# Two experts' endings rewritten: TensorE's branch moved ahead of them, the last half summed in PSUM, the first one's affine moved to other engines

## The chip, the core and the metric

One core of a Trainium2 chip runs one program with five engines: TensorE (PE, matmuls, results in PSUM), VectorE (DVE), ScalarE (ACT), GpSimd (POOL) and SyncE (SP, here the issuer of most DMAs). The time is device microseconds of one execution; the median over several runs counts. Weights stream from HBM during the whole program.

## The reference

Two hybrid layers (four mixers side by side) come first, then two blocks of attention and mixture of experts. All is in float32, for 256 tokens of 1024 channels. The change lies in the second part:

```python
x = layer_norm(DEEPNORM_ALPHA * x + (1 + g1) * y, ln_g[i, 0], ln_b[i, 0])   # y: attention (i=0 neighbourhood, i=1 grouped)
h = x * (1 + sc2) + sh2
y = hierarchical_moe(h, ...)            # 32 experts, 2 of them per token
x = layer_norm(DEEPNORM_ALPHA * x + (1 + g2) * y, ln_g[i, 1], ln_b[i, 1])
...                                     # the next block begins with
h = x * (1 + sc1) + sh1                 # sc1, sh1, g1: rows of mod = silu(c) @ ada_w[i] + ada_b[i]
y = gqa_mixer(h, ...)                   # q, k, v = h @ w_qkv; rms norm, rope, attention, w_o
```

`layer_norm` takes mean and variance over the 1024 channels, then `(x - mean) * rsqrt(var + 1e-5) * g + b`.

## The kernel before

Each engine has its program written out by hand, in the order in which it runs; semaphores (`filled(...)`: a PSUM result is there; `drained(...)`: it has been read and its bank is free) join them. The 256 tokens are two tiles (`t` = 0, 1) of 128 partitions, X[:, t, :]. There are 8 PSUM banks of 512 columns; `begin(b, name)` waits until bank b is free.

The 32 experts of a block run in 8 rounds (`q`) of four (`experts`). A round gathers up to 32 tokens for each expert, multiplies with gate and up (L920), transposes the hidden values (`hidden`), multiplies with the down weights, scales with the gate row g2 on VectorE (`YS`, L1062) and scatters the sums back to the tokens with a matmul (`combine`, L983) that VectorE adds to ACC, which is X. In the last round of a block the down weights come in five pieces: three rows f of four experts (`down_rows`, L965) and the two halves of the last row (`down_end`, L973). Between them TensorE spreads the gain and the shift of the layer norm over the partitions (`norm_row`, L888: a matmul of one row of ones), ScalarE copies them to `LN_OUT`. VectorE then adds the last sums to X, takes the statistics (BATCH_NORM_STATS2, `stats`), GpSimd computes the inverse root (L2261) and VectorE applies mean, root, gain and shift in four passes of 1024 columns (`last_norm`, L1070).

Should an expert get more than 32 tokens, `overflow` computes the rest. It stands under an `If` on the largest count (`cnt`): the engine loads the number (TENSOR_LOAD) and branches. `overflow` isn't entered for these inputs, but its code lies between: 32 experts written out. TensorE meets this `If` after the ending; VectorE before its own ending, which stands there twice (once with `overflow`, once in `Else`).

The grouped attention of the second block follows the first block's ending. TensorE first spreads the gate row g1 (`gate_rows`, L493, called by `common(1, "g")`), transposes X (`norm_cols`, L449), and once ScalarE (`early_cols`) and VectorE (`last_cols`) have scaled and shifted the transposed columns into `HT`, it multiplies with the keys' and the queries' weights: `k0` (L453, keys of tile 0), then `k1`, `q00`, transposes `K0`, `K1`, then `q10`, `r00` and the first scores. GpSimd computes the inverse roots of the keys' and queries' norms (`ROPED`). SyncE loads all large weights, each piece into the slot of an older one, after that has been used.

Of the kernel before, what the change touches and what calls it, by code (L numbers as in the profile page):

```python
# [9 lines left out]
ALU = mybir.AluOpType  # L10
# [4 lines left out]
NT = 2  # L15
# [113 lines left out]
def program(nc, A, out):  # L129
    with ExitStack() as ctx:  # L130
# [303 lines left out]
        def _(eng):  # L434
# [371 lines left out]
            def grouped():  # L806
# [83 lines left out]
            def experts(i):  # L890
# [12 lines left out]
                for q in range(NQ):  # L903
# [52 lines left out]

                    def down_rows():
                        o = [begin(5 + n, "dn", i, q, n) for n in range(2)]
                        for j in range(4):
                            pe.wait_ge(*drained("aT", i, q, j))  # L960
                        for f in range(3):
                            pe.wait_ge(*loaded("dn", i, q, "row", f))
                            for n in range(2):
                                for j in range(4):
                                    ins = eng.matmul(o[n][32 * j:32 * j + 32, :], AT[u][:, j, 32 * f:32 * f + 32],  # L965
                                                     rows_of_four(i, f)[:, j, 512 * n:512 * n + 512], start=f == 0, stop=False)
# [3 lines left out]
                    def down_end(o, n):  # L970
                        pe.wait_ge(*loaded("dn", i, q, "end", n))
                        for j in range(4):
                            ins = eng.matmul(o[n][32 * j:32 * j + 32, :], AT[u][:, j, 96:128], ends_of_four(i, n)[:, j, :],  # L973
                                             start=False, stop=True)
                        end(ins, "dn", i, q, n)
                        DONE["dn", i, q, "end", n] = filled("dn", i, q, n)

# [8 lines left out]
                    if q == NQ - 1:  # L986
# [6 lines left out]
                    else:  # L993
                        down(0)
                        down(1)
                        combine(0)
                    combine(1)
# [48 lines left out]
            for i in range(DEPTH):  # L1046
# [6 lines left out]
                pe.wait_ge(sem("cnt"), i + 1)  # L1053
                with eng.If(eng.value_load(cnt[0:1, NE:NE + 1]) > CAP):
                    overflow(i)

        @block.vector
        def _(eng):
# [392 lines left out]
            def last_cols():  # L1451
                v.wait_ge(*filled("nT", 1, 1, 1))
                for a in range(4):
                    c = 4 + a
                    ins = ts(HT[:, c, 128:256], bank("nT", 1, 1, 1)[:, 128 * a:128 * a + 128],
                             mod[:, 1, 8 + c:9 + c], ALU.mult, mod[:, 1, c:c + 1], ALU.add)
                    if a == 3:
                        free(ins, "nT", 1, 1, 1)
# [3 lines left out]
            def norm_columns(n, i, k):  # L1462
# [6 lines left out]
                v.tell(tt(COMB[:, n, 1], COMB[:, n, 1], sh, ALU.add), sem("comb"), i + 1)  # L1469
# [41 lines left out]
            def out_quarter(i, t, q):  # L1511
                o, f = slice(256 * q, 256 * q + 256), f"o{t}{q}"
                v.wait_ge(*drained("g1", i, 0))
                v.wait_ge(*drained("g1", i, 1))
                v.wait_ge(*filled(TAG[i], f))
# [13 lines left out]
            def side(i, tokens, more):  # L1529
                for f in tokens:  # L1530
# [11 lines left out]
                    elif kind == "n":  # L1542
                        norm_columns(2 * i, i, 3)
# [19 lines left out]
            def neighbourhood():  # L1563
# [11 lines left out]
                norm_columns(0, 0, 3)  # L1575
# [6 lines left out]
            def grouped():  # L1582
                last_cols()
# [7 lines left out]

# [129 lines left out]
            def experts(i, chosen):  # L1721
# [17 lines left out]
                for q in range(NQ):  # L1739
# [8 lines left out]
                    for j in range(4):  # L1748
# [25 lines left out]
                        if not q:  # L1774
                            extract(10 + i)
                            gate_rows(2 + i)
                    v.wait_ge(*filled("gsT", i, q))
# [37 lines left out]
                    def end():  # L1815
                        for n in range(2):
                            down(n)
                            combine(n)
# [3 lines left out]
                    kept = v.n, dict(v.past), v.last  # L1822
                    with eng.If(eng.value_load(cnt[0:1, NE:NE + 1]) > CAP):
                        end()
                        overflow(i)
                    v.n, v.past, v.last = kept
                    with eng.Else():
                        end()
# [40 lines left out]
            def last_norm(i):  # L1869
                for t in range(NT):  # L1870
                    deviation(t)
                for n in range(2):
                    for h in range(2):
                        v.wait_ge(*drained("row", 2 * i + 1, n, h))
                for t in range(NT):
                    v.step(stt(X[:, t, :], X[:, t, :], bn_a[:, t, 0:1], LN_OUT[0], ALU.subtract, ALU.mult))
                v.chain()
                for t in range(NT):
                    v.wait_ge(sem("lrs"), n_dev[0] - 1 + t)
                    ins = stt(X[:, t, :], X[:, t, :], st2[:, t:t + 1], LN_OUT[1], ALU.mult, ALU.add)  # L1880
                    if i + 1 < DEPTH:
# [717 lines left out]
```

## Time and profile before

| | us |
|---|---|
| median of 3 runs (lowest, highest) | 1532.74 (1531.36, 1538.42) |
| the profiled execution's own time | 1536.27 |
| its span | 1534.5 |
| TensorE busy | 1376.1 (90%) |
| VectorE, ScalarE, GpSimd busy | 547.8, 218.1, 85.4 |
| moved by DMA | 531.23 MB, mean 346 GB/s |

The span is cut by the page into 40 slices. In slices 15 to 23 and 31 to 38, in the two blocks' experts, DMA is full at about 426 GB/s, and the time goes with the weights; in between, in the attention of the second block (about 930 to 1070 us), DMA falls as low as 106 GB/s and TensorE and VectorE set the pace. The first experts' ending is at 905 to 934 us, the second one's at 1500 to 1531 us, where the program ends.

### The profile page before, as it was taken

Reading aid. Unit: us, or ns where it says so; the run is one execution under the profiler, and the core shown is the slowest. Engines: PE = TensorE matmul, PEld = TensorE weight load, DVE = VectorE, ACT = ScalarE, POOL = GpSimd, SP = SyncE. Lnnn points to the kernel's source line nnn. Section 1 sums busy time; section 2 is a strip of 40 time slices with the busy share of each in tenths; the row PEclk is TensorE's granted clock in tenths of the full one; section 3 lists DMA queues with packets and bytes.
Section 4 is the critical chain, followed back from the end, with each engine's and each line's share of the span. In section 5 each row is a group of like instructions: output and inputs, shape, how many; then the busy total and the mean of one; then the engine's idle time right before and its main releaser. Section 6 shows DMA issues by size and latency. Waiting matters only on the chain.

```text
span 1534.5 us, 28540 instructions
## 1 busy us (share of the span) xinstructions
PE 1376.1 (90%) x12866; PEld 874.1 (57%) x12866; DVE 547.8 (36%) x1251; ACT 218.1 (14%) x578; POOL 85.4 (6%) x91
## 2 busy tenths in 40 slices
PE   7999999999999998879879788878999798798796
PEld 4886488578886555436435443467665363354451
DVE  3596659665843221111111105583211111111113
ACT  3230123022332000000000001442100000000000
POOL 3100111000003000000000001100200000000000
PEclk9999999999999999889889999989999898898997
DMA  9657945778869999999999997237999999999994
GB/s 345 225 195 261 333 171 202 285 267 306 311 270 353 421 427 426 428 426 425 428 426 426 427 399 278 106 121 316 423 410 426 426 426 428 427 426 426 428 420 178
DMA packets 94552, 531.23 MB, mean 346 GB/s; under 512 B 5184, under 2 KB 7424, under 8 KB 70608
## 3 DMA queue, kind: packets, MB, share of 16 engines
q1 hardware_dynamic: 91264, 519.40, 83.8%
q0 software_dynamic: 3152, 9.86, 1.9%
q8 instruction: 105, 1.72, 0.4%
q14 instruction: 31, 0.25, 0.0%
HBM read 528.19 MB, written 1.05 MB: 345 GB/s over the span
## 4 chain that ended last, share of the span: by engine, by line
PE 61%; DMA 29%; DVE 7%; ACT 1%; issue 1%; DVEq 0%; SPq 0%; ACTq 0%
PE bk L453 26%; PE bk L920 16%; DMA AR<-in_moe_w_down 14%; DMA ring<-in_moe_w_down 14%; PE bk L952 8%; PE bk L983 4%; DVE mpart L1070 3%; PE bk L449 2%; PE bk L672 2%; ACT AR L1901 1%; PE bk L687 1%; DVE AR L1062 1%; PE bk L643 1%; DMA ring<-in_w_in 1%; DVE sm L1073 1%
## 5 line engine op out<-in xcount | busy, mean ns | idle before, releaser
L920 PE MATMUL bk<-ring,AR 128*32 128x128 f32 x4480 | 267.5, 409 | 3.1 <-DMA ring<-in_moe_w_up 3.1
L920 PE MATMUL bk<-AR 128*32 128x128 f32 x3712 | 223.0, 409 | 4.8 <-DMA AR<-in_moe_w_up 4.0
L1062 DVE TENSOR_TENSOR AR<-bk,AR 128x128 f32<-128x128 f32 (+2 forms) x106 | 41.3, 390 | 516.9 <-ACT AR L1901 450.4
L920 PEld LDWEIGHTS bk<-ring,AR 128*32 128x32 f32 x4480 | 175.4, 127 | 85.6 <-DMA ring<-in_moe_w_up 5.6
L453 PE MATMUL bk<-ring,AR 128*128 128x256 f32 (+2 forms) x736 | 214.3, 449 | 5.7 <-ACT AR L1901 2.6
L1901 ACT ACTIVATE AR<-bk 128x512 f32<-128x512 f32 (+4 forms) x182 | 75.3, 436 | 931.9 <-PE bk L920 755.9
L920 PEld LDWEIGHTS bk<-AR 128*32 128x32 f32 x3712 | 144.8, 127 | 75.3 <-DMA AR<-in_moe_w_up 6.2
L453 PEld LDWEIGHTS bk<-ring,AR 128*128 128x128 f32 x736 | 141.3, 195 | 71.4 <-issue 54.4
L952 PE MATMUL bk<-ring,AR 128*32 128x512 f32 x544 | 137.5, 704 | 43.1 <-DMA ring<-in_moe_w_down 43.1
L453 PE MATMUL bk<-AR,ring 128*128 128x256 f32 (+1 forms) x832 | 170.6, 364 | 1.6 <-DVE diag L1062 1.6
L453 PEld LDWEIGHTS bk<-AR,ring 128*128 128x128 f32 x832 | 147.4, 190 | 21.4 <-issue 3.5
L952 PE MATMUL bk<-AR 128*32 128x512 f32 x352 | 130.8, 714 | 27.4 <-DMA AR<-in_moe_w_down 27.4
L1070 DVE SCALAR_TENSOR_TENSOR mpart<-ring,ccol,mpart 128x512 f32<-128x512 f32 x168 | 130.3, 776 | 6.0
L1062 DVE TENSOR_TENSOR AR<-bk,mpart 128x512 f32<-128x512 f32 x32 | 22.1, 691 | 218.8 <-PE bk L952 191.4
L952 PEld LDWEIGHTS bk<-ring,AR 128*32 128x32 f32 x544 | 31.0, 126 | 103.3 <-DMA ring<-in_moe_w_down 57.8
L449 PE MATMUL bk<-cst,AR 128*128 128x128 f32 (+1 forms) x356 | 63.9, 292 | 22.6 <-DVE AR L1746 12.0
L449 PEld LDWEIGHTS bk<-cst,AR 128*128 128x128 f32 (+1 forms) x356 | 41.3, 142 | 57.3 <-issue 26.2
L453 PE MATMUL bk<-AR 128*128 128x128 f32 (+1 forms) x536 | 71.2, 292 | 0.6 <-DVE AR L1062 0.5
L952 PEld LDWEIGHTS bk<-AR 128*32 128x32 f32 x352 | 28.4, 127 | 72.5 <-DMA AR<-in_moe_w_down 38.5
L453 PEld LDWEIGHTS bk<-AR 128*128 128x128 f32 x536 | 65.9, 199 | 4.7 <-issue 2.6
L983 PE MATMUL bk<-AR 128*128 128x512 f32 x128 | 61.1, 619 | 5.0 <-DVE AR L1062 5.0
L643 PE MATMUL bk<-ring,AR 128*128 128x512 f32 x128 | 55.5, 594 | 0.0
(161 smaller groups left out, 892.0 us busy)
## 6 DMA issues: line engine op xcount, KB each, us to landing
ring<-in_moe_w_gate SPq DMA_DIRECT2D x36, 2048.0 KB, 30.0
ring<-in_moe_w_up SPq DMA_DIRECT2D x34, 2048.0 KB, 26.8
AR<-in_moe_w_up SPq DMA_DIRECT2D x30, 2048.0 KB, 29.6
ring<-in_moe_w_down SPq DMA_DIRECT2D x30, 2048.0 KB, 34.2
AR<-in_moe_w_gate SPq DMA_DIRECT2D x28, 2048.0 KB, 27.3
AR<-in_moe_w_down SPq DMA_DIRECT2D x26, 2048.0 KB, 34.0
ring<-in_ada_w SPq DMA_DIRECT2D x24, 2048.0 KB, 10.7
ring<-in_w_in SPq DMA_DIRECT2D x12, 2048.0 KB, 14.4
```

Source lines behind the costliest of these rows:

```text
L449: return eng.transpose(o, a, ident[0:k, 0:k])
L453: ins = eng.matmul(o, l, r, start=i == 0, stop=i == len(pairs) - 1)
L643: ins = eng.matmul(o[:, :], BIG[:, x, OUTS[m] + 128 * t:OUTS[m] + 128 * t + 128], w[:, 2 * m + x, :], start=k + x == 0, stop=k + x == 4)
L672: ins = eng.matmul(o[b][:, a * nk:(a + 1) * nk], g["q"][h][:, t * 128:(t + 1) * 128], g["k"][h][:, 0:nk], start=True, stop=True)
L687: ins = eng.matmul(o[64 * b:64 * b + 64, 128 * x:128 * x + 128], g["v"][2 * x + b][kt], ET[j % 2][:, (2 * b + x) * nkt + kt, :], start=kt ...
L920: ins = eng.matmul(o[32 * f:32 * f + 32, 128 * m:128 * m + 128], XG[u][:, c, 32 * j:32 * j + 32], w[:, c, f::4], start=c == 0, stop=c == N ...
L952: ins = eng.matmul(o[32 * j:32 * j + 32, :], AT[u][:, j, 32 * f:32 * f + 32], w, start=f == 0, stop=f == 3)
L983: end(eng.matmul(o[:, :], GST[u][:, 128 * t:128 * t + 128], YS[:, 512 * n:512 * n + 512], start=True, stop=True), "cb", i, q, n, t)
L1062: return eng.tensor_tensor(o, a, b, op)
L1070: return eng.scalar_tensor_tensor(out=o, in0=a, scalar=s, in1=b, op0=op0, op1=op1)
L1073: return eng.tensor_reduce(o, a, AX, op)
L1901: return eng.activation(o, a, f, **kw)
```

## The change

For both blocks:

- TensorE loads `cnt` and branches before the ending; the ending stands in both arms.
- The ending's last half (columns 512 to 1023) isn't added by VectorE. TensorE first puts ACC into PSUM through a matmul with the identity (`begin_sums`), the combine of this half adds to it in the same bank (`end_sums`), and VectorE takes the statistics from PSUM. The last half's down product is cut into quarters of 256 columns, in two banks, so that the scaling and the sums run by quarters.

After the first block's experts only:

- `last_norm(0)` makes `(x - mean) * root` alone, with four operations of 512 columns, half of them from PSUM. The gain and the shift of the norm are folded with sc1 and sh1 into columns (`norm_columns(1, 1, 0, "comb1", 1)`, computed in the first round) that ScalarE (`early_cols`, even halves) and VectorE (`odd_cols`, odd halves) apply to the transposed X.
- X itself gets gain and shift on GpSimd: two operations of 1024 columns for a tile, tile 0 before and tile 1 after the inverse root of `k0`; VectorE waits for it (`res`) when it adds the attention's output.
- The gate row g1 is spread after `r00` and no longer before the transposes.

```diff
@@ grouped(), TensorE
                 fill_bank[0] = [4, 5, 6, 7]
-                common(1, "g")
                 for t in range(NT):
                     norm_cols(1, t)
                 for f in ("k0", "k1", "q00", "K0", "K1", "q10", "r00"):
                     unit(f)
+                common(1, "g")
@@ experts(i), TensorE
+                    halves = ((0, (("dn", i, q, 0), 5, 0, 512)), (1, (("quarter", i), 6, 512, 256)), (1, (("dn", i, q, 1), 0, 768, 256)))
...
+                    def begin_sums():
+                        o = []
+                        for t in range(NT):
+                            o.append(begin((2, 3)[t], "cb", i, q, 1, t))
+                            pe.wait_ge(*drained("cb", i, q - 1, 1, t))
+                            eng.matmul(o[t][:, :], ident, ACC[:, t, 512:1024], start=True, stop=False)
+                        return o
+
+                    def end_sums(o):
+                        pe.wait_ge(*drained("gsT", i, q))
+                        for c0 in (0, 256):
+                            pe.wait_ge(*(drained("dn", i, q, 1) if c0 else drained("quarter", i)))
+                            for t in range(NT):
+                                ins = eng.matmul(o[t][:, c0:c0 + 256], GST[u][:, 128 * t:128 * t + 128],
+                                                 YS[:, 512 + c0:768 + c0], start=False, stop=c0 > 0)
...
+                    def ending():
+                        sums = begin_sums()
                         norm_row(2 * i + 1, 0, LN_OUT[0])
                         o = down_rows()
                         norm_row(2 * i + 1, 1, LN_OUT[1])
                         down_end(o, 0)
                         combine(0)
                         down_end(o, 1)
-                    else:
...
+                        end_sums(sums)
+
+                    pe.wait_ge(sem("cnt"), i + 1)
...
+                    with eng.If(eng.value_load(cnt[0:1, NE:NE + 1]) > CAP):
+                        ending()
+                        overflow(i)
...
+                    with eng.Else():
+                        ending()
@@ experts(i, ...), VectorE
-                    def end():
-                        for n in range(2):
-                            down(n)
-                            combine(n)
+                    def end(stored):
+                        down(0)
+                        combine(0)
...
+                        for k, name in enumerate((("quarter", i), ("dn", i, q, 1))):
+                            v.wait_ge(*filled(*name))
+                            free(tt(YS[:, 512 + 256 * k:768 + 256 * k], bank(*name)[:, 0:256], G2[1][:, 256 * k:256 * k + 256],
+                                    ALU.mult), *name)
+                        for t in range(NT):
...
+                                v.step(eng.bn_stats(bn_s[:, t, 1, :], o))
@@ last_norm(i, stored), VectorE
+                if not i:
+                    for t in range(NT):
+                        v.wait_ge(sem("lrs"), n_dev[0] - 1 + t)
...
+                            free(ts(X[:, t, 512:1024], bank("cb", i, NQ - 1, 1, t)[:, :], bn_a[:, t, 0:1], ALU.subtract,
+                                    st2[:, t:t + 1], ALU.mult), "cb", i, NQ - 1, 1, t)
+                        v.tell(ts(X[:, t, 0:512], X[:, t, 0:512], bn_a[:, t, 0:1], ALU.subtract, st2[:, t:t + 1], ALU.mult),
+                               sem("xn"), 3 + t)
+                    return
@@ GpSimd, after the first block
+            for t in range(NT):
+                for h in range(2):
+                    g.wait_ge(*filled("nT", 1, t, h))
+                g.step(tt(X[:, t, :], X[:, t, :], LN_OUT[0], ALU.mult))
+                g.chain()
+                g.tell(tt(X[:, t, :], X[:, t, :], LN_OUT[1], ALU.add), sem("res"), t + 1)
+                g.wait_ge(sem("gvar"), t + 1)
+                rsqrt(st2[:, 8 * t:8 * t + 4], st[:, 8 * t:8 * t + 4], "grs", t + 1)
```

TensorE's order before, from the last hidden transposes of an ending on (L888 spreads the norm's rows, L965 and L973 are the down weights, L983 is `combine`):

```order
L449 MATMUL bk<-cst,AR 128x128 x4
L888 MATMUL bk<-AR,ones 128x512 x2
L965 MATMUL bk<-ring,AR 32x512 x8
L965 MATMUL bk<-AR 32x512 x16
L888 MATMUL bk<-AR,ones 128x512 x2
L973 MATMUL bk<-ring,AR 32x512 x4
L983 MATMUL bk<-AR 128x512 x2
L973 MATMUL bk<-ring,AR 32x512 x4
L983 MATMUL bk<-AR 128x512 x2
L1054 TENSOR_LOAD cnt
L1054 COMPARE_AND_BRANCH
```

And the same place now (L987 is `begin_sums`, L967 and L977 the down weights, L1005 `combine`; the arm that runs, in `Else`, has the same rows as those behind the branch):

```order
L449 MATMUL bk<-cst,AR 128x128 x4
L1027 TENSOR_LOAD cnt
L1027 COMPARE_AND_BRANCH
L987 MATMUL bk<-X,cst 128x512 x2
L888 MATMUL bk<-AR,ones 128x512 x2
L967 MATMUL bk<-ring,AR 32x512 x4
L967 MATMUL bk<-ring,AR 32x256 x8
L967 MATMUL bk<-AR 32x512 x4
```

The load and the branch have moved from behind the last sums to ahead of everything that the ending does, and two matmuls of 512 columns were added behind them.

VectorE's order before, at the end of the arm that runs and in `last_norm(0)` (L1062 scales and adds, L1070 are the four passes, L1067 is `last_cols`):

```order
L1062 TENSOR_TENSOR AR<-bk,mpart 128x512
L1062 TENSOR_TENSOR X<-X,bk 128x512 x2
L1440 BN_STATS st<-X 128x6 x2
L1827 UNCONDITIONAL_BRANCH
L1447 BN_AGGR st<-st 128x2
L1066 TENSOR_SCALAR st<-st 128x1
L1447 BN_AGGR st<-st 128x2
L1066 TENSOR_SCALAR st<-st 128x1
L1070 SCALAR_TENSOR_TENSOR X<-X,st,AR 128x1024 x4
L1067 TENSOR_SCALAR AR<-bk,mod 128x128 x4
```

And now (L1094 scales, L1099 normalises and is `odd_cols`):

```order
L1094 TENSOR_TENSOR AR<-bk,mpart 128x256 x2
L1867 BN_STATS st<-bk 128x6 x2
L1479 BN_AGGR st<-st 128x2
L1098 TENSOR_SCALAR st<-st 128x1
L1479 BN_AGGR st<-st 128x2
L1098 TENSOR_SCALAR st<-st 128x1
L1099 TENSOR_SCALAR X<-bk,st 128x512
L1099 TENSOR_SCALAR X<-X,st 128x512
L1099 TENSOR_SCALAR X<-bk,st 128x512
L1099 TENSOR_SCALAR X<-X,st 128x512
L1877 UNCONDITIONAL_BRANCH
L1099 TENSOR_SCALAR AR<-bk,cst 128x128 x8
```

The two additions to X are gone, four passes of 1024 columns have become four of 512, and eight column operations stand where four were.

## Rows read from the trace of the kernel before

**Rows 1.** Instructions in order of time, TensorE, first experts' ending: start us, length us, group.

```profile
905.61 1.98 PE L888 MATMUL bk<-AR,ones 1*128 1x512 f32 x4
907.52 3.62 PE L965 MATMUL bk<-ring,AR 128*32 128x512 f32 x16
910.91 1.95 PE L965 MATMUL bk<-AR 128*32 128x512 f32 x16
914.75 1.92 PE L965 MATMUL bk<-AR 128*32 128x512 f32 x16 [1.89 <-DMA AR<-in_moe_w_down]
916.60 1.98 PE L888 MATMUL bk<-AR,ones 1*128 1x512 f32 x4
918.51 1.07 PE L973 MATMUL bk<-ring,AR 128*32 128x512 f32 x8
920.48 1.96 PE L983 MATMUL bk<-AR 128*128 128x512 f32 x4 [0.91 <-DVE AR L1062]
...
925.01 1.99 PE L983 MATMUL bk<-AR 128*128 128x512 f32 x4 [1.57 <-DVE AR L1062]
931.91 2.08 PE L493 MATMUL bk<-diag,ones 64*128 64x512 f32 x4 [4.92 <-issue]
933.92 3.68 PE L449 MATMUL bk<-cst,X 128*128 128x128 f32 x16
938.19 20.89 PE L453 MATMUL bk<-ring,AR 128*128 128x512 f32 x48 [0.59 <-ACT AR L1901]
```

**Rows 2.** The same view, SyncE, around its own branch.

```profile
900.62 0.51 SPq L2495 DMA_DIRECT2D ring<-in_moe_w_down  x1
906.91 4.69 SPq L2404 DMA_DIRECT2D ring<-in_gqa_w_qkv  x1
```

**Rows 3.** The same view, TensorE, second experts' ending.

```profile
1500.69 3.01 PE L888 MATMUL bk<-AR,ones 1*128 1x512 f32 x4
1503.62 3.64 PE L965 MATMUL bk<-ring,AR 128*32 128x512 f32 x16
1507.04 2.54 PE L965 MATMUL bk<-AR 128*32 128x512 f32 x16
1509.96 1.92 PE L965 MATMUL bk<-AR 128*32 128x512 f32 x16 [0.38 <-DMA AR<-in_moe_w_down]
...
1515.69 3.38 PE L983 MATMUL bk<-AR 128*128 128x512 f32 x4 [0.90 <-DVE AR L1062]
```

**Rows 4.** Windows, TensorE: stretch us, length, busy (count), granted clock, DMA, GB/s.

```profile
907.60:911.00 3.40, 3.40 (x20) 0.50 1.05 396
911.00:927.00 16.00, 11.62 (x64) 1.00 1.02 373
...
931.60:938.20 6.60, 5.70 (x21) 0.50 1.05 389
...
1501.50:1508.30 6.80, 6.80 (x27) 0.50 0.96 366
```

**Rows 5.** Instructions in order of time, VectorE, first experts' ending.

```profile
924.28 0.68 DVE L1062 TENSOR_TENSOR AR<-bk,mpart 128x512 f32<-128x512 f32 x1
...
928.95 0.21 DVE L1447 BATCH_NORM_AGGREGATE st<-st 128x2 f32<-128x12 f32 x1
...
929.71 5.00 DVE L1070 SCALAR_TENSOR_TENSOR X<-X,st,AR 128x1024 f32<-128x1024 f32 x4
937.64 1.37 DVE L1067 TENSOR_SCALAR AR<-bk,mod 128x128 f32<-128x128 f32 x4 [2.93 <-PE bk L449]
```

**Rows 6.** The same view, GpSimd, last normalisation, then the affine of attention's normalisation.

```profile
929.43 1.97 POOL L2261 TENSOR_TENSOR st<-st,half 128x1 f32<-128x1 f32 x2 [25.19 <-DVE st L1066]
...
1085.11 4.78 POOL L2257 TENSOR_TENSOR X<-X,AR 128x1024 f32<-128x1024 f32 x2
```

**Rows 7.** The same view, VectorE, a scaling of 512 columns without PSUM.

```profile
1011.98 0.48 DVE L1066 TENSOR_SCALAR mpart<-ring,ccol 128x512 f32<-128x512 f32 x1
```

**Rows 8.** The same view, TensorE, at the scores after the first queries' transposes.

```profile
968.75 1.14 PE L672 MATMUL bk<-AR 64*128 64x256 f32 x8 [1.49 <-ACT AR L1901]
```

More of the change, by code:

```diff
@@ L955, in down @@
                         end(ins, "dn", i, q, n)
+                    halves = ((0, (("dn", i, q, 0), 5, 0, 512)), (1, (("quarter", i), 6, 512, 256)), (1, (("dn", i, q, 1), 0, 768, 256)))
                     def down_rows():
-                        o = [begin(5 + n, "dn", i, q, n) for n in range(2)]
+                        o = [begin(b, *name)[:, 0:c] for n, (name, b, c0, c) in halves]
                         for j in range(4):
@@ L1813, in experts @@
                         continue
-                    def end():
-                        for n in range(2):
-                            down(n)
-                            combine(n)
+                    def end(stored):
+                        down(0)
+                        combine(0)
+                        v.wait_ge(*filled("cb", i, q - 1, 1, 1))
+                        for k, name in enumerate((("quarter", i), ("dn", i, q, 1))):
[3 more added lines that the diff above has]
+                        for t in range(NT):
+                            o = bank("cb", i, q, 1, t)[:, :]
+                            v.wait_ge(*filled("cb", i, q, 1, t))
+                            if stored:
+                                free(eng.tensor_copy(ACC[:, t, 512:1024], o), "cb", i, q, 1, t)
+                                v.chain()
+                                v.step(stats(t, 1, ACC))
+                            else:
+                                v.step(eng.bn_stats(bn_s[:, t, 1, :], o))
                     v.wait_ge(sem("cnt"), i + 1)
-                    kept = v.n, dict(v.past), v.last
+                    kept = v.n, dict(v.past), v.last, n_dev[0]
                     with eng.If(eng.value_load(cnt[0:1, NE:NE + 1]) > CAP):
-                        end()
+                        end(True)
                         overflow(i)
-                    v.n, v.past, v.last = kept
+                        last_norm(i, True)
+                    v.n, v.past, v.last, n_dev[0] = kept
                     with eng.Else():
-                        end()
+                        end(False)
+                        last_norm(i, False)
             def overflow(i):
@@ L2371, in _ @@
                 deviation(t)
-            for n, f in enumerate(ROPED):
-                o = slice(8 * (n % 2), 8 * (n % 2) + (4 if f[0] == "k" else 8))
+            for n in range(2):
+                for h in range(2):
+                    g.wait_ge(*drained("row", 1, n, h))
+            for t in range(NT):
+                for h in range(2):
+                    g.wait_ge(*filled("nT", 1, t, h))
[4 more added lines that the diff above has]
+                rsqrt(st2[:, 8 * t:8 * t + 4], st[:, 8 * t:8 * t + 4], "grs", t + 1)
+            for n in range(2, len(ROPED)):
+                o = slice(8 * (n % 2), 8 * (n % 2) + 8)
                 g.wait_ge(sem("gvar"), n + 1)
```

97 lines of the change are left out of this document (54 added, 43 removed).

## The prediction

> **What bounds the kernel now.** I read the page first (shares, slices), then the instructions of each engine in order of time around both endings, the chain of waits through them, and last the granted clock by windows. In the experts the weights' stream is full, so little on the engines counts there. What counts is what stands behind the last large weights: the first ending up to `k0`, and the second ending up to the program's end.
>
> At the first ending TensorE is at the edge of that cover. The last row of down weights lands at 914.7, and TensorE has been idle for 1.89 us by then [rows 1]. All before it is hidden by no more than this. In the second ending the same wait is only 0.38 us [rows 3]. Behind it comes a chain: norm row, first half of the last row, scaling, `combine(0)`, second half, scaling (924.28), `combine(1)` until 927.0, VectorE's last sum, statistics and four passes until 934.7, and then the transposes and scaled columns until `k0` starts at 938.19 [rows 1, 5]. TensorE's own branch lies beside that: after its last sum it starts nothing for 4.92 us, at 931.91 it spreads the gate row, at 933.92 it transposes. X of tile 0 is normalised after three of VectorE's four passes, at 929.71 + 3 x 1.25 = 933.5. So before, branch plus gate row ended 0.4 us behind the normalisation: the branch was as good as hidden, by VectorE's work. The question is what hides it in front of the ending. Only the 1.89 us and the 0.38 us do.
>
> **The branch ahead.** Its cost is not shown at the new place, so it is bounded by rows. From the end of TensorE's last sum (927.0) to its next matmul it is 4.9 us; counted from the start of that combine (925.01), after which the sequencer could already have gone on to the load, it is 6.9 us [rows 1]. SyncE's own load and branch on the same number stand between 901.13 and 906.91, 5.8 us [rows 2]. I take 5.8 us, near the middle; the ends 4.9 and 6.9 are kept for the range. The Trainium skill, "Runtime: NRT & Kernel Launch", section "Instruction fetch mechanics", says that a taken branch outside the fetched pages waits for a DMA of its target; the rows agree in that both engines stand for about 5 us. The same skill's "Advanced Engine Details and Errata", section "Control Flow Timing", has compare-and-branch at about 108 ns; by that alone nothing would be lost here, and it is weighed below as a rival. The unconditional jump at the end of `Else` is new on TensorE; VectorE has such a jump before, between its statistics and the aggregate at 928.95 [rows 5], and no gap is there, so I count it as nothing (it also lies in the wait for VectorE).
>
> **First ending, up to the row that was awaited.** Before, from 905.61 to the end of that row at 916.67: 11.1 us. After: branch 5.8. Then `begin_sums`, two matmuls of 512 columns, 4 records. At full clock four such cost 1.96, at half clock 3.38 [rows 1, 3]. The clock was granted at 0.50 (1.2 GHz) from 907.6 to 911.0, after the short gaps of the last transposes, and from 931.6 to 938.2, after the 4.9 us of idle; otherwise at 1.00 (2.4 GHz) [rows 4]. An idle branch in front makes the low clock likely, so 3.4. Then the norm's row 1.9, and three rows of weights. A row costs 1.92 at full clock and 3.62 at half [rows 1]; before, the first one had the half clock. Its quarters of 256 columns may cost a little more than halves of 512: between nothing and 0.25 us per row, I take 0.13. Three rows: 6.15. Sum 5.8 + 3.4 + 1.9 + 6.15 = 17.25, so the row ends 17.25 - 11.1 = 6.2 us later. This is the largest term, and the 1.89 us of slack is already used in it.
>
> **First ending, the chain behind.** (a) From the half's scaling to the last sum it was 927.0 - 924.28 = 2.7 us: 0.68 and a combine of 1.99. By quarters the second scaling lies beside the first sums: about 2.4, gain 0.3. (b) From the last sum to the normalised tile 0 it was 933.5 - 927.0 = 6.5: VectorE finished two additions to X (0.7 left), two statistics 1.28, four small operations until 929.71, three passes of 1.25 [rows 5]. Now: the statistics begin at once, 1.1 until both are there, 0.4 for the first pair of small ones, one inverse root 1.0 (two are 1.97 [rows 6]), then one operation of 512 from PSUM at about 0.7 (as the scaling from PSUM at 924.28) and one from SBUF at 0.48 [rows 7]: 3.7. Gain 2.8. (c) From there to `k0` it was 938.19 - 933.5 = 4.7: 0.4 for TensorE, a tile's transposes 1.8 (3.68 for two [rows 1]), and ScalarE's two row copies and eight column operations. Now ScalarE has four columns and VectorE the other four (1.37 [rows 5]), after the second tile's normalisation, which ends 1.2 us after the first one's: about 3.2. Gain 1.5. (d) The gate row now lies between the transposes `r00` and the first scores, where TensorE waited for 1.49 us [rows 8]; it costs 2.08, so 0.6 us comes back there. Its two copies on ScalarE fall in that wait too. (e) GpSimd's affine: 2 x 2.4 = 4.8 us per tile [rows 6]. Tile 0 starts when its transposes are done, about 2 us after the norm, and is over at about 7; the root of `k0` is asked for some 12 us after the norm (3.2, a product of 20.89 / 3 = 7.0 [rows 1], its copy and square). Tile 1's 4.8 us and a root of 1.0 fit into the 7.0 us of `k1`. Nothing, with about a microsecond to spare for the second. `norm_columns` is three operations of 0.15 under the weights' stream. Nothing.
>
> Sum for the first ending: 6.2 - 0.3 - 2.8 - 1.5 + 0.6 = +2.2 us. It is passed on: until about 990 us DMA has gaps, and the next experts' weights go into slots that the attention's matmuls free.
>
> **Second ending.** Before, from 1500.69 to the end of the awaited row at 1511.88: 11.2 us, with the norm's row at 3.01 and the first two rows at 3.42 and 2.54 for the half clock of 1501.5 to 1508.3 [rows 3, 4]. After: 5.8, 3.4, 2.6 for the norm's row (between 1.9 and 3.01), 6.15: 17.95, so +6.75. Behind it, `combine(0)` ran at half clock before, 3.38 against 1.96 [rows 3, 1]; with what the quarters give I take -1.0 (bounds -0.3 and -1.7). From the last sum to the last pass: the addition of 0.7 goes, the passes become four of 0.7 and two of 1.25, 5.3 for 5.0: -0.5. Sum +5.2 us.
>
> **The clock.** Norm rows use one partition, and in the second ending the clock stayed low through such a row and a whole row of weights behind it, until 1508.3 [rows 3, 4]. In the new order each ending has a norm's row soon after the idle branch, so a further stretch of 3.4 us at half clock behind it is about as likely as not in each; one costs half of it, 1.7 us. I count one of the two: +1.7. Bounds 0 and 5.1, as the clock could also stay low into `k0`.
>
> **Sum.** 2.2 + 5.2 + 1.7 = +9.1 us. The profiled span of 1534.5 becomes about 1543.6; that execution took 1536.27 in all, within 0.3% of the median 1532.74. On the median: 1541.8 us, 0.6% slower.
>
> **Rivals.**
> A. The branch is nearly free in front. For it: the 108 ns of the skill's page; the 4.92 us are called "issue", which names no cause. Against: SyncE shows 5.8 us at its own branch, and nothing else stands between TensorE's sum and its next matmul. In this case both terms lose 5.8 us and the extra low clock: 9.1 - 11.6 - 1.7 = -4.2, about 1528.5 us. The gain and the loss change over at 9.1 - 1.7 = 7.4 for two branches of 5.8, so at 2.1 us for one branch: below that the kernel is not slower. Chance 0.18 for not slower at all. More than 0.5% faster (under 1525) would need the shorter chain to be worth 3.5 us more as well, say `k0` starting right behind the transposes.
> B. The change costs as worked out but with the low ends: branch 4.9, clock not low again. 9.1 - 1.8 - 1.7 = +5.6, 1538.3 us: within 0.5%. For it: at 911 us the clock came back while the first row of weights ran. Against: in the second ending it did not. Chance 0.23.
> C. The clock stays low for long: every norm row, `begin_sums` and the first keys at 0.50, branch 6.9: 9.1 + 2.2 + 3.4 = +14.7, 1547.4 us. Chance 0.12.
> D. The chain behind gains nothing, because VectorE's operations on PSUM or GpSimd's 4.8 us beside VectorE are slower than in the rows, or the roots come late by GpSimd's affine: (b) and (c) are lost, +4.3, 1546 us. Chance 0.05.
>
> **How the numbers follow.** My own case, +6 to +12 around 1541.8, has 0.42. About 0.5%, 7.7 us or 1540.4, is what a measurement of this kernel can tell from no change. Slower by more than that: C, D and three quarters of my case, 0.48. Faster by more than that: the tail of A, 0.06. Within: the rest, 0.46. The range leaves out the lower part of A and the upper end of C: 1531 to 1547.
>
> **What would show it.** TensorE: a gap of 5 to 7 us after the last hidden transposes (905.7) and again at about 1501, where before there was none, and the last row of weights without a wait for its DMA; that gap gone between the last sum and the transposes. VectorE: no additions to X between the last scaling and the statistics; normalised tile 0 about 3.7 us after the last sum instead of 6.5. `k0` at about 940 instead of 938.2, the program's end about 9 us later. If the gap in front is under 2 us, the forecast is wrong from its first step; if it is there and `k0` still starts before 938, the chain behind was worth more than I found in it.

## The result, and the profile after

| | before | changed |
|---|---|---|
| median us, as the two were timed together (6 runs each) | 1534.18 | 1548.47 |
| lowest to highest | 1531.36 to 1538.48 | 1540.46 to 1554.21 |
| profiled execution: its own time, span | 1536.27, 1534.5 | 1547.22, 1545.4 |
| ratio to before, 95% interval | | 1.0083 (1.0056 to 1.0109) |
| ratio, timed once more (`e0_changed`) | | 1.0081 (1.0054 to 1.0108) |

The change makes the kernel 0.8% slower. Applied to the 1532.74 us shown ahead, the ratio gives 1545.5, 12.7 us more; the forecast was 1541.8, 9.1 us more. In `e8_before_round6` below, and for the kernel before timed beside it, one execution each (1814 and 1967 us, at a mean granted clock of 0.645 and 0.555) is left out of the ratios as slow.

The first experts' ending on TensorE in the changed kernel, instructions in order of time (start us, length us, group, and in brackets the idle time before it):

```profile
903.55 0.33 PE L449 MATMUL bk<-cst,AR 128*128 128x128 f32 x1 [0.52 <-DVE AR L1814]
910.26 3.66 PE L987 MATMUL bk<-X,cst 128*128 128x512 f32 x4 [6.38 <-issue]
913.85 1.98 PE L888 MATMUL bk<-AR,ones 1*128 1x512 f32 x4
915.76 1.93 PE L967 MATMUL bk<-ring,AR 128*32 128x512 f32 x24
917.51 3.63 PE L967 MATMUL bk<-AR 128*32 128x512 f32 x48
921.07 1.98 PE L888 MATMUL bk<-AR,ones 1*128 1x512 f32 x4
...
929.20 1.99 PE L995 MATMUL bk<-AR 128*128 128x256 f32 x8 [1.30 <-DVE AR L1094]
934.53 3.43 PE L449 MATMUL bk<-cst,X 128*128 128x128 f32 x16 [3.34 <-DVE X L1099]
938.06 20.84 PE L453 MATMUL bk<-ring,AR 128*128 128x512 f32 x48
```

Against [rows 1]: the 4.92 us between the last sum and the next matmul have become 3.34, and these are a wait for VectorE; 6.38 us stand in front instead, where the norm's row followed the transposes at once. The 1.89 us of waiting for the last row of weights are gone, since TensorE comes too late for it. The second ending, same view:

```profile
1508.36 3.78 PE L987 MATMUL bk<-X,cst 128*128 128x512 f32 x4 [6.25 <-issue]
1512.07 3.78 PE L888 MATMUL bk<-AR,ones 1*128 1x512 f32 x4
1515.78 3.64 PE L967 MATMUL bk<-ring,AR 128*32 128x512 f32 x24
1519.19 4.64 PE L967 MATMUL bk<-AR 128*32 128x512 f32 x48
```

Against [rows 3]: a gap of 6.25 us, and then everything up to 1521 at half the clock. The granted clock, windows with TensorE alone (stretch us, length, busy time and count, granted clock, DMA share, GB/s):

```profile
907.00:913.60 6.60, 3.34 (x4) 0.50 0.98 362
913.70:934.30 20.60, 15.29 (x117) 1.00 1.04 383
...
1504.40:1521.10 16.70, 12.74 (x44) 0.50 0.47 179
```

The clock fell to 1.2 GHz during both gaps. In the first ending it was back at 913.6; in the second it stayed down for 16.7 us, where before, without a gap, it was down for 6.8 [rows 4]. VectorE at the first ending, same kernel:

```profile
928.74 0.74 DVE L1094 TENSOR_TENSOR AR<-bk,mpart 128x256 f32<-128x256 f32 x2
930.80 1.30 DVE L1867 BATCH_NORM_STATS2 st<-bk 128x6 f32<-128x512 f32 x2 [1.32 <-PE bk L995]
...
933.21 0.81 DVE L1099 TENSOR_SCALAR X<-bk,st 128x512 f32<-128x512 f32 x1 [0.26 <-POOL st L2323]
933.94 0.54 DVE L1099 TENSOR_SCALAR X<-X,st 128x512 f32<-128x512 f32 x1
...
936.54 2.82 DVE L1099 TENSOR_SCALAR AR<-bk,cst 128x128 f32<-128x128 f32 x8 [0.69 <-PE bk L449]
```

No additions to X between the last scaling and the statistics, which come straight from PSUM, and tile 0 is normalised at 934.48, 3.3 us after the last sum at 931.2; before, it was 6.5 us, with three passes of 1.25 us in them [rows 5]. So the new chain works; it starts too late.

To compare kernels I read two stretches from each profile, since the times at which the endings are reached differ by some microseconds from run to run: from the end of the last hidden transposes to the start of `k0`, and from the end of the same transposes in the second block to the end of VectorE's last pass. These are 903.88 to 938.06 and 1502.11 to 1542.22 here, 905.68 to 938.19 and 1500.76 to 1531.34 before. Each row of the table is one profiled execution, beside the ratio of many.

| kernel | first | second | sum | ratio to before (95%) |
|---|---|---|---|---|
| before | 32.5 | 30.6 | 63.1 | |
| changed | 34.2 | 40.1 | 74.3 | 1.0083 (1.0056 to 1.0109) |
| changed again, `e0_changed` | 40.2 | 33.8 | 74.1 | 1.0081 (1.0054 to 1.0108) |
| branch behind, `e1_behind` | 30.2 | 31.9 | 62.2 | 0.9984 (0.9968 to 1.0000) |
| before, branch ahead, `e2_before_ahead` | 40.1 | 36.8 | 76.9 | 1.0100 (1.0078 to 1.0122) |
| branch a round ahead, `e3_round7` | 25.9 | 25.9 | 51.8 | 0.9988 (0.9972 to 1.0004) |
| arms swapped, `e4_swapped` | 29.4 | 30.3 | 59.7 | 0.9979 (0.9960 to 0.9997) |
| near arm, `e5_short` | 35.2 | 28.4 | 63.6 | 0.9988 (0.9965 to 1.0011) |
| branch two rounds ahead / behind, `e6_round6` | 29.6 | 28.2 | 57.8 | 0.9960 (0.9943 to 0.9977) |
| the same once more, `e9_round6_again` | 27.5 | 29.2 | 56.7 | 0.9958 (0.9939 to 0.9977) |
| norm row later, `e7_rows_first` | 38.5 | 36.1 | 74.6 | 1.0078 (1.0048 to 1.0109) |
| before, that place, `e8_before_round6` | 34.2 | 31.9 | 66.1 | 1.0013 (0.9996 to 1.0030) |

The changed kernel's sum is 11.2 and 11.0 us over before in two profiles, most of the 12.7. The sums follow the ratios to within 2.5 us. Only in `e3_round7` does the sum mislead: there TensorE is late already when the stretch begins. What the first ending loses is passed on to the end: from `k0` to the second block's last hidden transposes it is 562.6 us before, 564.1 and 563.9 in the changed kernel's two profiles, and 562.3 to 566.0 in all but `e3_round7`, whose second branch lies in that stretch, however long the first ending was.

### The profile page after: what moved, and what is told of

Its sections match the earlier page's. It is cut to its first block, busy times and chain, and to the rows that moved or that the text cites. A ratio compares the mean times of both kernels' runs of the same rounds, so it can differ in the third digit from the quotient of the medians.

```text
span 1545.4 us, 28707 instructions
## 1 busy us (share of the span) xinstructions
PE 1381.3 (89%) x12946; PEld 883.1 (57%) x12946; DVE 550.6 (36%) x1258; ACT 216.6 (14%) x574; POOL 93.4 (6%) x95
## 4 chain that ended last, share of the span: by engine, by line
PE 61%; DMA 28%; DVE 8%; issue 2%; ACT 1%; SPq 0%; DVEq 0%; POOL 0%; ACTq 0%
PE bk L453 26%; PE bk L920 16%; DMA ring<-in_moe_w_down 14%; DMA AR<-in_moe_w_down 9%; PE bk L952 8%; DMA ring<-in_moe_w_up 4%; DVE mpart L1102 3%; PE bk L1005 3%; PE bk L449 2%; PE bk L672 1%; DVE AR L1094 1%; PE bk L687 1%; ACT AR L1965 1%; PE bk L643 1%; PE bk L967 1%
## 5 line engine op out<-in xcount | busy, mean ns | idle before, releaser
L1094 DVE TENSOR_TENSOR AR<-bk,AR 128x128 f32<-128x128 f32 (+2 forms) x106 | 41.3, 389 | 515.7 <-ACT AR L1965 450.1
L453 PE MATMUL bk<-ring,AR 128*128 128x256 f32 (+2 forms) x736 | 210.1, 443 | 4.9 <-ACT AR L1965 2.0
L1094 DVE TENSOR_TENSOR AR<-bk,mpart 128x512 f32<-128x512 f32 (+1 forms) x34 | 22.2, 658 | 235.2 <-PE bk L952 190.9
L453 PE MATMUL bk<-AR 128*128 128x128 f32 (+1 forms) x536 | 74.3, 301 | 0.5 <-DVE AR L1094 0.4
L453 PEld LDWEIGHTS bk<-AR 128*128 128x128 f32 x536 | 69.0, 207 | 4.6 <-issue 2.5
L952 PEld LDWEIGHTS bk<-AR 128*32 128x32 f32 x352 | 28.3, 126 | 71.7 <-DMA AR<-in_moe_w_down 38.5
L1005 PE MATMUL bk<-AR 128*128 128x512 f32 x120 | 57.1, 618 | 1.8 <-DVE AR L1094 1.8
```

What stands on the lines that cost most here:

```text
L453: ins = eng.matmul(o, l, r, start=i == 0, stop=i == len(pairs) - 1)
L952: ins = eng.matmul(o[32 * j:32 * j + 32, :], AT[u][:, j, 32 * f:32 * f + 32], w, start=f == 0, stop=f == 3)
L1005: end(eng.matmul(o[:, :], GST[u][:, 128 * t:128 * t + 128], YS[:, 512 * n:512 * n + 512], start=True, stop=True), "cb", i, q, n, t)
L1094: return eng.tensor_tensor(o, a, b, op)
```

## The experiments

### The branch back behind the ending

```diff
-                    with eng.If(eng.value_load(cnt[0:1, NE:NE + 1]) > CAP):
-                        ending()
-                        overflow(i)
-                    with eng.Else():
-                        ending()
+                    ending()
+                    with eng.If(eng.value_load(cnt[0:1, NE:NE + 1]) > CAP):
+                        overflow(i)
```

> The changed kernel with TensorE's load and branch back behind the ending; all else as changed. Theory: the branch is the whole loss (the gap of 6.3 us twice and the half clock that follows it). Then the gaps of 6.3 us after the last hidden transposes are gone, the second ending falls from 40 us (last hidden transposes to last pass) to about 31, and what is left is the shorter chain, 3 to 4 us, less about 1.4 us because the branch, now begun with the last sums, ends later than the normalisation: 3 us faster than before, ratio 0.998 (0.995 to 1.000). Rival: the loss comes from the new work (the identity matmuls, quarters, PSUM operands, GpSimd's affine). Then the kernel stays slower than before, ratio 1.005 or more.

Ratio 0.9984 (0.9968 to 1.0000). TensorE in order of time:

```profile
905.32 1.88 PE L987 MATMUL bk<-X,cst 128*128 128x512 f32 x4
...
915.04 1.93 PE L967 MATMUL bk<-AR 128*32 128x512 f32 x24 [2.35 <-DMA AR<-in_moe_w_down]
...
925.04 1.99 PE L995 MATMUL bk<-AR 128*128 128x256 f32 x8 [1.30 <-DVE AR L1090]
932.20 3.37 PE L449 MATMUL bk<-cst,X 128*128 128x128 f32 x16 [5.16 <-DVE X L1095]
```

The identity matmuls follow the transposes at once and run at full clock; the weights are waited for again (2.35 us), so the identity matmuls are free at this place. The gap behind the last sum is 5.16 us where VectorE alone needed 3.34: the branch behind costs 1.8 us now that the chain beside it is shorter (the profile names VectorE there, but X of tile 0 is normalised by 930.3). All of the loss is the branch's place; the rival falls.

### Before, with the branch alone moved

The ending of the kernel before is written in both arms, ahead of it the load and the compare.

> The kernel before with one part of the change alone: TensorE's load and branch stand ahead of the ending, which is written out in both arms; no sums in PSUM, no quarters, everything else as before. Theory (the branch is the loss): a gap of 6.3 us in front of each ending, 1.9 and 0.4 us of it covered by the wait for the weights, half clock behind it; +4 to +5 us in the first, +7 to +9 in the second ending, ratio 1.007 to 1.010. Rival (the new work is the loss): ratio 0.999 to 1.002.

Ratio 1.0100 (1.0078 to 1.0122), the two endings 7.6 and 6.2 us longer than before. TensorE, both endings:

```profile
909.44 3.78 PE L888 MATMUL bk<-AR,ones 1*128 1x512 f32 x4 [6.46 <-issue]
...
1513.60 3.78 PE L888 MATMUL bk<-AR,ones 1*128 1x512 f32 x4 [6.26 <-issue]
```

This one part of the change costs 1% alone, the upper end of what was expected (the first ending longer than that, the second shorter). The clock is low behind both gaps: the norm's row takes 3.78 us, against 1.98 in [rows 1] and 3.01 in [rows 3].

### The branch a round earlier

The last round became a function `one_round(q)`, written in both arms:

```diff
+                for q in range(NQ - 1):
+                    one_round(q)
+                with eng.If(eng.value_load(cnt[0:1, NE:NE + 1]) > CAP):
+                    one_round(NQ - 1)
+                    overflow(i)
+                with eng.Else():
+                    one_round(NQ - 1)
```

> The changed kernel with TensorE's load and branch another 35 us earlier, at the start of the last round of four experts, where TensorE leads the weights' stream; the round is written out in both arms. Theory: the gap of about 6.3 us is still there, but TensorE needs 7.7 us for an expert's gate and up for which the stream needs 9.8, so it catches up within the round, the clock has recovered, and neither ending nor the normalisation sees the branch: the whole gain of the rest shows, 4 to 6 us faster than before, ratio 0.9965 (0.994 to 0.999). Rival (the new work is the loss): ratio 1.005 or more. Second rival: the late freed slots make a gap in the weights' stream, as long as the branch: ratio 1.004 or more with a DMA share under 0.95 somewhere behind the branch.

Ratio 0.9988 (0.9972 to 1.0004): the loss is gone, but the gain, 0.9965 as expected, isn't shown. TensorE, the two branches, and the weights of the first ending:

```profile
873.27 7.58 PE L919 MATMUL bk<-AR 128*32 128x128 f32 x128 [4.80 <-issue]
...
911.47 3.63 PE L966 MATMUL bk<-AR 128*32 128x512 f32 x48
```

```profile
1466.18 3.84 PE L919 MATMUL bk<-AR 128*32 128x128 f32 x62 [3.73 <-issue]
1471.88 4.04 PE L919 MATMUL bk<-AR 128*32 128x128 f32 x65 [1.85 <-issue]
```

At 911.47 both last rows run without a wait for DMA: one round isn't quite enough to catch up. The DMA share stayed at 0.99 or more behind both branches, in slices of 10 us up to the last weights, so the second rival falls too. In the second block another idle of 1.85 us follows 3.8 us after the first one of 3.73, again without a wait that the profile names; probably more code that was late, but no run tells.

The clock fell in these gaps as well (granted 0.50 from 874 to 876), but there it costs nothing: from 873.3 to 877.0, at a mean of 0.55, 68 of these small matmuls ran in 3.7 us, and from 877 to 884, at 1.00, 128 in 7.0, the same pace.

### The arms swapped

```diff
-                    with eng.If(eng.value_load(cnt[0:1, NE:NE + 1]) > CAP):
+                    with eng.If(eng.value_load(cnt[0:1, NE:NE + 1]) <= CAP):
                         ending()
-                        overflow(i)
                     with eng.Else():
                         ending()
+                        overflow(i)
```

> The changed kernel with the arms swapped on TensorE: the condition is at most 32, so the arm that runs stands right behind the compare and the jump over the other arm (32 experts of code) comes at its end. Theory: the 6.3 us are the wait for far code after a taken branch; the load and a branch not taken cost under 1.5 us, so the gap in front falls to 0.5 to 1.5 us, and a gap of about 6 us from the last sums' issue appears behind the first ending, as in the kernel before; ratio 0.998 to 1.001. Rival: the time is the load of the number and the compare, wherever the arm lies: the gap in front stays at 6 us and the ratio at 1.007 to 1.010.

Ratio 0.9979 (0.9960 to 0.9997). TensorE, first ending, then second:

```profile
902.07 3.62 PE L987 MATMUL bk<-X,cst 128*128 128x512 f32 x4 [0.43 <-issue]
...
927.49 3.67 PE L449 MATMUL bk<-cst,X 128*128 128x128 f32 x16 [4.53 <-issue]
```

```profile
1494.43 1.98 PE L987 MATMUL bk<-X,cst 128*128 128x512 f32 x4 [0.18 <-issue]
```

The wait for the count's semaphore, the load and the compare are still in front, at the same place, and cost 0.43 and 0.18 us. The gap has gone with the taken jump to where that now stands, behind the last sum (4.53 us in the first ending). So the 6.3 us are not the load of the number, and not a wait for that semaphore: they belong to the jump over 32 experts of code.

### The near arm

`overflow(i)` is left out of TensorE's program (it isn't entered for these inputs); the jump is still taken, over one copy of the ending.

> The changed kernel with one thing left out: TensorE's copy of the code for more than 32 tokens per expert, which isn't entered for these inputs. Load, compare and a taken branch stay ahead of the ending, but the arm in Else now stands right behind one copy of the ending instead of 32 experts of code further on. Theory: the 6.3 us are the wait for far code; a taken branch over a few hundred instructions is much cheaper, the gap falls under 3 us, ratio 0.997 to 1.002. Rival: a taken branch costs 6 us wherever it goes, because what was fetched ahead is dropped: gap 6 us, ratio 1.006 to 1.010.

Ratio 0.9988 (0.9965 to 1.0011), gaps of 1.40 and 0.53 us. TensorE, first ending, and its clock in that stretch:

```profile
904.33 3.78 PE L987 MATMUL bk<-X,cst 128*128 128x512 f32 x4 [1.40 <-issue]
908.04 3.78 PE L888 MATMUL bk<-AR,ones 1*128 1x512 f32 x4
911.75 3.64 PE L967 MATMUL bk<-ring,AR 128*32 128x512 f32 x24
```

```profile
904.30:920.00 15.70, 15.67 (x81) 0.58 1.00 372
```

A taken jump is cheap when its target is near, 1.40 and 0.53 us against 6.3: the distance makes the price. The Trainium skill ("Runtime: NRT & Kernel Launch", section "Instruction fetch mechanics") says that code is fetched in order, and that a jump out of the fetched window waits for a DMA of its target; the trace agrees in that only the far jump is dear, while that DMA itself is in no view shown here. The same skill has compare-and-branch at about 108 ns ("Advanced Engine Details and Errata", section "Control Flow Timing"); that leaves room in the 0.18 and 0.43 us of the branch that isn't taken, load included, and does not describe the far one. The second fence shows something else: the clock was low here for most of 15.7 us although the gap was only 1.4 us and TensorE busy throughout. Identity matmuls, norm row and weights took 15.5 us here and 10.8 in the first ending of the swapped arms, which is most of why the first ending is long (35.2 against 29.4).

### Two rounds ahead in the first block, behind in the second

```diff
+                if i:
+                    for q in range(NQ):
+                        one_round(q)
+                    with eng.If(eng.value_load(cnt[0:1, NE:NE + 1]) > CAP):
+                        overflow(i)
+                    return
+                for q in range(NQ - 2):
+                    one_round(q)
...                                  # If/Else as above, with both last rounds in each arm
```

> A version meant to beat both: the changed kernel with TensorE's branch of the first block two rounds ahead (at the start of the last but one round, both rounds written out in both arms) and of the second block behind its ending, where nothing follows. Theory: the gap is caught up within two rounds under the weights' stream, neither ending sees it: last hidden transposes to k0 about 28 us (32.5 before, 30.4 with the branch behind), 5 us faster than before, ratio 0.996 (0.994 to 0.998). Rival: the weights' stream is what is left and no branch place is worth more than another: ratio 0.998 to 0.999, the same as with the branch behind.

> The changed kernel with TensorE's branch two rounds ahead in the first block and behind the ending in the second, once more, on the same chip and beside the same runs of the kernel before as the kernel before with that place alone. Theory: 0.996 again (0.994 to 0.998), and 0.003 to 0.004 below that kernel. Rival: the first measurement was luck of the chip, and both come out alike.

Ratios 0.9960 (0.9943 to 0.9977) and 0.9958 (0.9939 to 0.9977): faster than before by 0.4%, than the changed kernel by 1.2%. TensorE in the first of the two, at the branch, at the weights of the first ending, at `k0`:

```profile
814.12 11.35 PE L919 MATMUL bk<-ring,AR 128*32 128x128 f32 x192 [4.31 <-issue]
```

```profile
911.81 1.93 PE L966 MATMUL bk<-AR 128*32 128x512 f32 x24 [1.85 <-DMA AR<-in_moe_w_down]
...
932.32 13.04 PE L453 MATMUL bk<-ring,AR 128*128 128x512 f32 x27
```

The gap is still there at 810, but 1.85 us of waiting for the last weights' row show that TensorE has caught up. In the second ending nothing follows the branch. This is the fastest version of all; its interval overlaps that of the swapped arms (0.9960 to 0.9997), which also beat both kernels.

### Before, with that place of the branch alone

> The kernel before with nothing changed but the place of TensorE's branch: in the first block two rounds ahead of the ending, in the second behind it as it was. Theory: before, the branch lay beside VectorE's passes and reached 0.4 us over them, so freeing the tail of it is worth 0.4 us: ratio 0.999 to 1.001; what the version with both gains is then the rest of the change (sums in PSUM, normalised only, columns on both engines), about 4 us. Rival: the gain of that version is the branch's new place itself: ratio 0.995 to 0.998 here too.

Ratio 1.0013 (0.9996 to 1.0030): no gain, as expected by the theory; timed beside the same executions of the kernel before, the changed kernel with the same place was at 0.9958. In this profile a second idle stretch of 3.91 us follows the one of 4.14 at the branch, as in the second block of `e3_round7`; TensorE still waited 2.28 us for the last weights' row, so it had caught up. That its first ending is 1.7 us longer than before comes from `combine(0)`, which ran at half the clock here (3.62 us against 1.96 in [rows 1]). So the place alone is worth nothing to the kernel before, where the branch lay beside VectorE's passes, and the 0.4% are the rest of the change (the last half in PSUM, tile 0 normalised only, the columns on two engines). Which part of it they belong to, no run separates.

### The norm's row behind the weights

```diff
-                        norm_row(2 * i + 1, 0, LN_OUT[0])
                         o = down_rows()
+                        norm_row(2 * i + 1, 0, LN_OUT[0])
                         norm_row(2 * i + 1, 1, LN_OUT[1])
```

> The changed kernel with the first norm row moved behind the three rows of weights, so that the identity matmuls and the weights follow the idle branch without the one-partition matmuls of the norm row between them. Theory (such a matmul does not bring the clock back): the half clock of the second ending, 1504.4 to 1521.1, ends some 7 us earlier, the ending is 3 to 4 us shorter, ratio 1.005 to 1.007. Rival (the order of these does not matter to the clock): the half clock lasts as long as in the changed kernel, ratio 1.008 to 1.010.

Ratio 1.0078 (1.0048 to 1.0109): not to be told from the changed kernel's, and the interval also holds the 1.005 to 1.007 of the theory. TensorE, first ending:

```profile
914.39 3.11 PE L967 MATMUL bk<-ring,AR 128*32 128x512 f32 x24
...
920.87 4.66 PE L888 MATMUL bk<-AR,ones 1*128 1x512 f32 x8
925.46 1.93 PE L977 MATMUL bk<-ring,AR 128*32 128x512 f32 x8
928.30 3.75 PE L1005 MATMUL bk<-AR 128*128 128x512 f32 x4 [0.91 <-DVE AR L1094]
```

The clock came back during the weights but fell again behind the two norm rows, and the half of a row after them ran at half the clock (1.93 us against 1.06). In the second ending it was back some 4 us after the gap, as the theory wants, and the ending took 36.1 us, between the changed kernel's 40.1 and 33.8 without the new order. As long as two profiles of one kernel differ by that much, one of this can't decide. My reason for the size of that term (the norm row keeps the clock down) isn't shown by this.

### The changed kernel again

> The changed kernel itself once more, on the same chip as the others and beside the kernel before: every theory expects a ratio of 1.006 to 1.011, a gap of 6 to 6.5 us in front of each ending, and the half clock in the second one for 7 to 17 us.

Ratio 1.0081 (1.0054 to 1.0108). TensorE, first ending:

```profile
913.72 3.78 PE L987 MATMUL bk<-X,cst 128*128 128x512 f32 x4 [6.46 <-issue]
917.43 3.78 PE L888 MATMUL bk<-AR,ones 1*128 1x512 f32 x4
921.14 3.64 PE L967 MATMUL bk<-ring,AR 128*32 128x512 f32 x24
```

Here it is the first ending in which the clock stays low through norm row and weights (40.2 us), and the second is short of that (33.8). The first profile had it the other way round; the sum is the same.

## Why the prediction was right, and where its sizes were off

The kernel got slower by more than 0.5%, to which the prediction gave 0.48 against 0.46 for no change that can be told, and 1545.5 us lies near the upper end of its range, 1531 to 1547.

- **The step that decides** was right: the branch was hidden before and isn't in front. Its size was taken too small. Measured 6.38 and 6.25 us, taken 5.8 with ends at 4.9 and 6.9. Of the two ways to count the old gap, the one from the start of the last combine (6.9) was the better. The idle time alone differs by what runs ahead of the jump: 4.92 and 4.53 us (before, swapped arms) behind 2 us of combine, 6.20 to 6.46 behind a transpose of 0.33. Counted from the start of that last group all are alike, 6.5 to 6.9 us, so part of the jump's price passes beside the matmuls issued ahead of it.
- **First ending up to the awaited row**: forecast 17.25 us, measured 903.88 to 921.14, 17.26. That this agrees so well is luck, since the terms inside were off against each other: the gap 0.6 longer, the identity matmuls 0.2, the three rows 5.4 instead of 6.15; quarters cost nothing extra.
- **The chain behind**: scaling to last sum 2.4 (forecast 2.4), last sum to tile 0 normalised 3.3 (3.7), from there to `k0` 3.6 (3.2). Together right. `k0` was forecast at about 940 and starts at 938.06, because this execution reached the ending 1.8 us earlier than the one before; the first stretch is longer by 1.7 us, and without the gate row, which lies outside of it, the forecast for it was 1.6.
- **The gate row** was forecast to cost 0.6 us at its new place; from the start of `r00`'s transposes to the scores it was 2.1 before and is 2.0 now, so it cost nothing. At full clock it takes 1.13 us; the 2.08 in [rows 1] were at half clock, which I had read and not used. TensorE, changed kernel:

```profile
966.48 0.60 PE L449 MATMUL bk<-cst,AR 128*128 128x128 f32 x4
967.01 1.13 PE L493 MATMUL bk<-diag,ones 64*128 64x512 f32 x4
968.48 1.13 PE L672 MATMUL bk<-AR 64*128 64x256 f32 x8 [0.34 <-ACT AR L1965]
```

- **Second ending up to the awaited row**: forecast 17.95 us, measured 1502.11 to 1523.83, 21.7. This is the mis-sized term. Identity matmuls 3.7, norm row 3.7 instead of 2.6, three rows 8.0 instead of 6.15, all by the half clock until 1521.1. Behind it, to the last sum, 0.3 us came back instead of 1.0: `combine(0)` ran at half clock again (3.33 us; 3.38 before).
- **The clock** was counted as one further stretch in both endings, 1.7 us. In the profile the half clock puts the terms of the second ending, without its gap, at 15.5 us instead of 12.15, so 3.3 us where 1.7 were counted; in the repeated profile it falls on the first one. This and the larger gaps (2 x 0.5 us) are more than what lies between 9.1 and the two profiled sums of 11.2 and 11.0; the shorter rows of the first ending and the free gate row took some of it back.
- **Rival A**, the branch nearly free in front, fell by the gaps of 6.3 us, but its reason was half right: a branch that isn't taken costs next to nothing. **Rival D** (1546 us) comes closest by its number and is wrong by its mechanism: VectorE was slowed beside GpSimd, but off the path (below), and the shorter chain kept its gain. **B** and **C** differ from my case by the clock and the length of the gap; the measured time lies between mine and C's 1547.4, nearer to C.

## What to carry to other kernels

The jump over 32 experts of code cost TensorE 6.5 to 6.9 us here, counted from the start of the last matmuls ahead of it, and each gap of 6.2 to 6.5 us was followed by half the clock. Put such a jump where that engine leads its weights by more than this, let the arm that runs stand right behind the compare, and ask of each branch what covers it now before moving it. A version that looks worse by one part may hold a gain in the rest. Here the rest is worth 0.4% with the branch two rounds ahead and then behind; at the other places without the loss the ratio was 0.9979 to 0.9988, and only that of the swapped arms is clear of 1.

## What the hardware showed that was not expected

VectorE was held up while GpSimd worked. GpSimd, then VectorE, changed kernel, in order of time, and last VectorE at the same place before:

```profile
936.68 4.78 POOL L2319 TENSOR_TENSOR X<-X,AR 128x1024 f32<-128x1024 f32 x2 [2.97 <-PE bk L449]
...
947.98 4.82 POOL L2319 TENSOR_TENSOR X<-X,AR 128x1024 f32<-128x1024 f32 x2
```

```profile
939.29 3.20 DVE L1094 TENSOR_TENSOR AR<-cst,qkn 128x64 f32<-128x64 f32 x8
...
948.04 2.56 DVE L1094 TENSOR_TENSOR AR<-AR,st 128x256 f32<-128x256 f32 x1 [1.14 <-POOL st L2323]
950.64 3.45 DVE L1094 TENSOR_TENSOR AR<-AR 128x128 f32<-128x128 f32 x6
```

```profile
948.22 0.43 DVE L1062 TENSOR_TENSOR AR<-AR,st 128x256 f32<-128x256 f32 x1 [1.13 <-POOL st L2261]
948.68 1.43 DVE L1062 TENSOR_TENSOR AR<-AR 128x128 f32<-128x128 f32 x6
```

The operation at 948.04 took 0.43 us before and now ends at 950.6, just behind the end of GpSimd's first operation (947.98 + 2.4); the six behind it took 1.43 before and now 3.45, 2.32 of them the first one's, which ends just behind GpSimd's second. The eight column operations of 2.82 us, which read one operand from PSUM, were not slowed (1.37 for four before [rows 5]). The Trainium skill, "SBUF — State Buffer", section "Who interferes with whom", says that a VectorE instruction with two SBUF inputs contends with a GpSimd instruction that reads SBUF, by an exclusive lock on the ports that the two share; the trace agrees. It cost nothing here: VectorE was done with these keys at 954.6, and TensorE, busy with other matmuls, took up their transposes 20.7 us after the start of `k0`, as before (938.06 to 958.74; 938.19 to 958.92).

The low clock varies from one execution to the next in the same kernel: some 7 us in one ending and 16.7 in the other in one profile, and the other way round in its repeat. After a gap of 6.2 to 6.5 us it was low in all eight endings that were profiled with one. It was low for a while in endings without such a gap too ([rows 4]; 3.62 us for the identity matmuls of the swapped arms; the 15.7 us of the near arm), so how much of the low clock the gap brings, and how long it stays, is open.
